# A mixture-of-experts layer: the hidden product written in column order, its transposes reading every fourth column

## What is computed

```python
def expert_block(args):
    xb, e = args
    return (jax.nn.silu(xb @ w_gate[e]) * (xb @ w_up[e])) @ w_down[e]
...
y_assign = out_rows[dest] * sw[:, None].astype(out_rows.dtype)
y = jax.ops.segment_sum(y_assign, st, num_segments=n_tok)
```

## Time and profile before

| | us |
|---|---|
| median of three runs | 1308.99 |
| the profiled execution, its own time | 1305.18 |
| its span in the profile | 1303.4 |
| TensorE busy | 1142.9 (88%) |
| VectorE busy | 825.9 (63%) |
| ScalarE busy | 647.6 (50%) |
| GpSimd busy | 298.3 (23%) |

### The profile page before, as it was taken

How to read it: one execution, slowest core, us unless ns; L and a number is a source line. 1 busy time by engine, 2 the same in 40 slices (tenths; PEclk the granted TensorE clock), 3 DMA queues, 4 the chain that set the end, 5 groups by cost and what they waited for, 6 DMA issues and landing times. The chain is left out here.

```text
span 1303.4 us, 15836 instructions
## 1 busy us (share of the span) xinstructions
PE 1142.9 (88%) x5652; PEld 876.9 (67%) x5652; DVE 825.9 (63%) x871; ACT 647.6 (50%) x850; POOL 298.3 (23%) x409
## 2 busy tenths in 40 slices
PE   4899988978978977999549999999999999999984
PEld 3787967857957955888436666666666666666652
DVE  6232445454554555534457899997888888888861
ACT  5112135244244236222226777776676767677751
POOL 4113415524514503100000211111111111111030
PEclk9899989989969967999759999999999999999997
DMA  6410201001000032225559999999999999999931
GB/s 185 113 48 0 66 1 49 16 0 48 16 0 0 0 129 53 97 97 182 206 212 312 347 361 375 367 369 349 356 360 365 367 361 371 363 365 369 372 122 18
DMA packets 88768, 253.81 MB, mean 195 GB/s; under 512 B 13632, under 2 KB 38224, under 8 KB 80528
## 3 DMA queue, kind: packets, MB, share of 16 engines
q1 hardware_dynamic: 81392, 236.23, 49.8%
q0 software_dynamic: 7328, 16.94, 5.9%
HBM read 240.55 MB, written 20.97 MB: 201 GB/s over the span
## 5 line engine op out<-in xcount | busy, mean ns | idle before, releaser
L1569 DVE TENSOR_TENSOR wlo<-raw,whi 128x2048 fp32r<-128x2048 f32 x192 | 433.6, 2285 | 87.2 <-ACT whi L1524 79.3
L1524 ACT CAST whi<-raw 128x2048 fp32r<-128x2048 f32 x186 | 345.7, 1910 | 0.0
L1649 PE MATMUL banks<-whi,rT_hi 128*96 128x512 f32 x512 | 166.2, 406 | 11.9 <-PE banks L1675 8.8
L1653 PE MATMUL banks<-whi,rT_lo 128*96 128x512 f32 x512 | 160.7, 395 | 0.0
L1651 PE MATMUL banks<-wlo,rT_hi 128*96 128x512 f32 x512 | 160.3, 394 | 0.0
L1504 POOL DMA_INDIRECT out<-y_sb,table_i x32 | 55.0, 1720 | 304.2 <-ACT y_sb L1542 304.2
L1528 ACT CAST rT_hi<-banks 128x384 fp32r<-128x384 f32 x64 | 30.8, 481 | 180.3 <-PE banks L1625 180.3
L1649 PEld LDWEIGHTS banks<-whi,rT_hi 128*96 128x96 f32 x512 | 76.0, 163 | 47.9 <-issue 21.3
L1651 PEld LDWEIGHTS banks<-wlo,rT_hi 128*96 128x96 f32 x512 | 83.0, 162 | 36.2
L1653 PEld LDWEIGHTS banks<-whi,rT_lo 128*96 128x96 f32 x512 | 83.1, 162 | 35.8
L1495 POOL DMA_INDIRECT rows<-xn_rows,table_i x30 | 47.3, 1576 | 219.6 <-PE banks L1625 206.8
(11 more groups left out here) (257 smaller groups left out, 2128.7 us busy)
## 6 DMA issues: line engine op xcount, KB each, us to landing
raw<-in_w_gate SPq DMA_DIRECT2D x128, 512.0 KB, 7.8
raw<-in_w_up SPq DMA_DIRECT2D x128, 512.0 KB, 10.5
raw<-in_w_down SPq DMA_DIRECT2D x64, 1024.0 KB, 10.0
q_raw<-in_w_in SPq DMA_DIRECT2D x12, 512.0 KB, 5.7
x_all<-in_x SPq DMA_DIRECT2D x4, 1024.0 KB, 9.6
z_raw<-in_w_in SPq DMA_DIRECT2D x8, 512.0 KB, 5.2
wo_raw<-in_w_out SPq DMA_DIRECT2D x2, 2048.0 KB, 10.5
x_again<-in_x SPq DMA_DIRECT2D x8, 512.0 KB, 4.0
```

Source lines behind the costliest of these rows:

```text
L1524: act.copy(s.w_hi[i % HI][:], s.raw[i % RING][:]).then_inc(s.hi_ready, 1)
L1569: dve.tensor_tensor(s.w_lo[i % RING][:], s.raw[i % RING][:], s.w_hi[i % HI][:].bitcast(F32), ALU.subtract).then_inc(s.lo_ready, 1)
L1649: pe.matmul(ps[0:SLOTS, bank + g, :], s.rT_hi[e % 2][:, c, :], hi[:, g, c2, :], start=(c == 0), stop=False)
L1653: ins = pe.matmul(ps[0:SLOTS, bank + g, :], s.rT_lo[e % 2][:, c, :], hi[:, g, c2, :], start=False, stop=(c == KC - 1))
```

## The change

`hid` becomes a plain tile of 96 partitions by 512 elements. The product, in `hidden` and in its copy in `spare_blocks`, reads and writes in the order of the columns. Each transpose takes its 128 columns of the stationary operand with a step of four elements (16 bytes) instead of in a row. Nothing else changes: not the number of instructions, nor their order, nor a wait.

```diff
-        hid = [at(f"hid{b}", 172 + 2 * b, [SLOTS, FC, P]) for b in range(2)]
+        hid = [at(f"hid{b}", 172 + 2 * b, [SLOTS, FF]) for b in range(2)]
...
             def hidden(e):
                 dve.wait_ge(silu_ready, e + 1)
-                dve.scalar_tensor_tensor(s.hid[e % 2][:].rearrange("s c p -> s p c"),
-                                         s.silu[:].rearrange("s (p c) -> s p c", c=FC), s.table_w[:, e:e + 1],
-                                         ps[0:SLOTS, gate_banks(e) + 1, :].rearrange("s (p c) -> s p c", c=FC),
-                                         ALU.mult, ALU.mult).then_inc(hid_ready, 1)
+                dve.scalar_tensor_tensor(s.hid[e % 2][:], s.silu[:], s.table_w[:, e:e + 1],
+                                         ps[0:SLOTS, gate_banks(e) + 1, :], ALU.mult, ALU.mult).then_inc(hid_ready, 1)
...
                 for c in range(FC):
-                    ins = pe.transpose(ps[:, 5, c * P:c * P + SLOTS], s.hid[e % 2][:, c, :], s.ident[0:SLOTS, 0:SLOTS])
+                    ins = pe.transpose(ps[:, 5, c * P:c * P + SLOTS], s.hid[e % 2][:, c:FF:FC], s.ident[0:SLOTS, 0:SLOTS])
                 ins.then_inc(hid_turned, 1)
```

More of the change, by code:

```diff
@@ L1803, in body @@
                 dve.wait_ge(spare_weight, i + 1)
-                dve.scalar_tensor_tensor(s.hid[0][:].rearrange("s c p -> s p c"),
-                                         s.silu[:].rearrange("s (p c) -> s p c", c=FC), s.w_spare[:],
-                                         ps[0:SLOTS, 1, :].rearrange("s (p c) -> s p c", c=FC),
+                dve.scalar_tensor_tensor(s.hid[0][:], s.silu[:], s.w_spare[:], ps[0:SLOTS, 1, :],
                                          ALU.mult, ALU.mult).then_inc(spare_hid, 1)
@@ L1830, in body @@
                 for c in range(FC):
-                    ins = pe.transpose(ps[:, 6, c * P:c * P + SLOTS], s.hid[0][:, c, :], s.ident[0:SLOTS, 0:SLOTS])
+                    ins = pe.transpose(ps[:, 6, c * P:c * P + SLOTS], s.hid[0][:, c:FF:FC], s.ident[0:SLOTS, 0:SLOTS])
                 ins.then_inc(spare_hid_turned, 1)
```

## The result

The changed kernel takes 1312.9 us, the median of seven runs (1311.07 to 1317.28), against 1308.99 us before (seven runs as well, 1306.79 to 1309.80). The ratio is 1.0038 with an interval of 1.0024 to 1.0053: slower, by 3.9 us in the medians, less than half a percent. The forecast was 1313, slower, in a range of 1307 to 1322.

What follows compares the result with a forecast made beforehand. The expert stage was taken as bound by TensorE's instruction rate. VectorE's saving counted 0 and exposed transpose loads 3 x 48 x 31 ns, 4.5 us, so 1308.99 + 4.5 = 1313.5, rounded to 1313 us, range 1307 to 1322.

Steps and rivals of the forecast that it cites:

- TensorE's stream is the limit, and a nanosecond added to a transpose is added to the kernel: Expert stage: bound by the rate at which TensorE takes instructions, 18.5 us per expert; added transpose time reaches the end.
- VectorE's saving is off the path: Product of `hid` on VectorE: 1132 to 752 ns, 32 times, 12.2 us saved, of which 0 reaches the end.
- The rival that it comes through: VectorE's saved time returns, 0.38 us per expert, up to 12.2 us, 1297 us at the most; chance 0.07.
- A contiguous load occupies 54 ns of an 81 ns distance: Transposes of `hid` on TensorE: the stationary load takes about 54 of 81 ns between starts, leaving 27 ns spare.
- fixed 84 ns: Part of a load's record not growing with columns, derived from rounded-type loads of 96 and 128 columns (162 and 188 ns).
- The load with a step: Transposes' loads with 16-byte steps: 54 ns becomes 108 to 150 ns; the middle taken, 48 ns showing per exposed load.
- Three of four loads show, and the last expert's are free: Transposes of `hid`: first load hides under a large matmul, last expert's under a 4.58 us wait; 3 x 48 x 31, 4.5 us.
- The load's record would grow towards 190 to 230 ns: Profile sign at the transposes of `hid`, line 1633: the load record grows from 138 ns towards 190 to 230.
- The nearest row was VectorE's scattered store: Stepped loads priced from VectorE's scattered access: ratio 1.7 (about 108 ns) or 0.75 ns per element (150 ns).
- The rule of the lines: SBUF access in 16-byte lines, full speed needing two hits per line; speaks against the transposes' 16-byte step, names no size.
- slower: Whole-kernel outcome: time rises, +2.5 to +6.4 us as forecast or 1321.6 us with four-fold loads; chance 0.52 together.
- no change: Whole-kernel outcome within about 0.2%, 2.6 us: free reads (chance 0.36) plus some 0.05 from the cheaper reading; chance 0.41.

Runs made afterwards that it cites:

- the product alone: Changed kernel with contiguous product but transposes reading 128 columns in a row as before, against the kernel before: 1308.97 us, ratio 0.9996 (0.9987 to 1.0005).

## Why the prediction was right

- *TensorE's stream is the limit, and a nanosecond added to a transpose is added to the kernel.* Right: 0.11 us more in the chain's group, 0.114 us more per expert, 3.5 us for 31, of the 3.9 us measured; the other 0.4 us is within the scatter of the runs.
- *VectorE's saving is off the path.* Right, and shown by the product alone (0.9996). Predicted 752 ns, measured 736; its idle time grew by 10.6 us where about 10 were forecast. The rival that it comes through is refuted.
- *A contiguous load occupies 54 ns of an 81 ns distance.* It fits the measurement, but its fixed 84 ns are worked out from records of other loads, of the rounded type, so the split is an inference. The distance is measured.
- *The load with a step.* This term was mis-sized. I took 129 ns for the distance (48 over the 81), the middle of 108 and 150. Measured are 115 and 120 ns, some 37 over. The forecast for the group was 0.48 us, it is 0.44; for the sum 4.5 us, it is 3.5.
- *Three of four loads show, and the last expert's are free.* Three is right in number: three distances grew, 3 x 37 ns = 0.111 us, and the first load's longer record (0.20 against 0.14 us) costs nothing. With all four under large matmuls the step costs nothing at all; behind a drained queue all four show. The last group is followed by a wait of 4.41 us for `wlo`, as the row says; a kernel with only that group changed wasn't run.

```profile
1268.09 0.69 PE L1631 MATMUL banks<-ident,hid 96*128 96x96 f32 x4 [0.30 <-PE banks L1673]
1273.19 1.14 PE L1669 MATMUL banks<-whi,hidT_hi 128*96 128x512 f32 x2 [4.41 <-DVE wlo L1569]
```

- *The load's record would grow towards 190 to 230 ns.* It is 195 to 223.
- *The nearest row was VectorE's scattered store.* Right in sign, and near in size by chance only. It was a poor guide to the mechanism: as a ratio it gave 1.7, and the transposes' loads went, by the same inferred split, from 54 to some 112 to 118 ns, about double, while the loads of the large matmuls hardly changed.
- *The rule of the lines.* The Trainium skill, Advanced Engine Details and Errata, section SBUF Cachelines, has the sign right for a step of four. Its condition of two hits isn't borne out for these loads: with a step of two each 16-byte line gets two hits, and the record is 214 ns, nearly that of a step of four. The Trainium skill, TensorE: Matmul & The Clock Gate, section LDWEIGHTS, gives 0.83 ns a column. Less the fixed 84 ns, the records agree closely for the rounded type (0.81, and 0.86 with a step) and for the plain load of 96 columns (0.84). A transpose's loads with a step are above it, 0.91 set apart and 0.95 to 1.05 in a row, and its contiguous load is far below, at 0.44. That figure knows no step, so by it the loads, and the time, would have stayed as they were.

The chance given to this case with slower was 0.52 and to no change 0.41. That was a fair reading: the effect, 0.30 to 0.38%, is just above what can be told, and a load 37 ns shorter would have hidden it all.

## What to carry to other kernels
On an engine that is the bound, look at the distance between its instructions and at which side of each sets it: by the split above, these transposes had some 27 ns of cover for their loads, so a load some 60 ns longer (201 against 141 ns, both set apart) cost 37. Put transposes whose operand is read with a step between long matmuls (of 230 ns here), not in a row, and the step is free; but then check who must be ready earlier, above all while the pipeline fills, for kernels with the wait moved to the front of a tile lost 2 to 4 us here. A faster instruction on an engine that has slack was worth nothing: 12.7 us of VectorE moved this kernel by less than its intervals can tell.

## What the runs showed of the hardware
The unexpected part is how flat the price of a step is. Take the fixed 84 ns of the prediction from each record; the figures per column rest on it, the records don't. A transpose's contiguous load of 128 columns then has 56 ns, 0.44 a column; with a step of four it has 201 - 84 = 117 ns, 0.91 a column (set apart, with a large matmul on each side); steps of two, three and eight lie within 12 ns of that of four in a row (214, 210 and 206 against 218 ns). The rounded type's load of 96 columns has 78 ns contiguous and 83 with a step of two, 0.81 and 0.86 a column. So these runs look as if all loads went at some 0.8 to 1.0 ns a column, save the contiguous load of a transpose, which goes twice as fast, and each of the four steps tried takes that speed away. Why contiguous loads of transposes are faster stays open. A pattern of adjacent pairs with gaps between, which would tell whether adjacency or a single run is needed, wasn't run.
